# Two chained sequence models on one core: squares and sums of the norms in four parts, projections between the heads of the second model's mixers, and the last expert's residual handed over by pairs

## What is computed

```python
proj = h @ w_in
c_q, c_kv, k_rope, q_m, k_m, v_m, o_m, i_m, f_m, g_mla, g_mlstm = jnp.split(proj, split_at, axis=-1)
q = (_rmsnorm(c_q, q_norm_w) @ w_uq)...          # 8 heads, 64 + 32 (rotated)
kv = (_rmsnorm(c_kv, kv_norm_w) @ w_ukv)...      # 8 heads, 64 + 64
y_mla = _mla_attention(q_nope, q_rope, k_nope, k_rope, v)
qk = jax.nn.silu(_causal_dwconv(jnp.concatenate([q_m, k_m], axis=-1), conv_w, conv_b))
hm = _mlstm_chunkwise(q_m, k_m * 64 ** -0.5, v_m, i_pre, log_sigmoid(f_pre))
y_mlstm = jax.nn.sigmoid(o_m) * _rmsnorm(hm, head_norm_w)
merged = (jax.nn.sigmoid(g_mla) * (y_mla @ w_br_mla)
          + jax.nn.sigmoid(g_mlstm) * (y_mlstm @ w_br_mlstm))
return merged @ w_out
```

## Time and profile before

| | |
|---|---|
| time, three runs | 2615.55 us median, 2609.03 to 2618.73 |
| profiled execution | 2614.95 us |
| its span in the trace | 2613.1 us, mean granted clock 0.933 |
| TensorE busy | 2408.3 us (92%), 12979 matmul records |
| VectorE, ScalarE busy | 1620.1 us (62%), 1102.9 us (42%) |
| weights and inputs read | 575.26 MB, 221 GB/s over the span |
| second model's mixers | from 1473.66 to 1801.06 us and from 2046.06 us to 2374.4 us of the span |

### The profile page before, as it was taken

How to read it: one execution, slowest core, us unless ns; L and a number is a source line. 1 busy time by engine, 2 the same in 40 slices (tenths; PEclk the granted TensorE clock), 3 DMA queues, 4 the chain that set the end, 5 groups by cost and what they waited for, 6 DMA issues and landing times.

```text
span 2613.1 us, 31144 instructions
## 1 busy us (share of the span) xinstructions
PE 2408.3 (92%) x12979; PEld 2074.1 (79%) x12979; DVE 1620.1 (62%) x1728; ACT 1102.9 (42%) x1187; POOL 54.2 (2%) x101
## 2 busy tenths in 40 slices
PE   1988998987999999999999799998999999898997
PEld 1777998776888888888888686687898786687996
DVE  3574875335898898898899232423888223334674
ACT  0233442415666676766666122112444122113552
POOL 1000000000000000000000000000000000000000
PEclk9979998987999999999999996699999895899998
DMA  8753986423999999999999451043887350143551
GB/s 283 268 192 108 335 303 222 145 81 128 369 377 366 360 378 372 356 376 373 374 365 369 118 151 33 15 146 99 310 276 234 98 162 1 49 145 98 193 184 42
DMA packets 338882, 578.38 MB, mean 221 GB/s; under 512 B 48082, under 2 KB 208810, under 8 KB 326450
## 3 DMA queue, kind: packets, MB, share of 16 engines
q1 hardware_dynamic: 324738, 474.65, 53.2%
q0 software_dynamic: 13824, 100.67, 9.9%
q10 hardware_dynamic: 176, 1.02, 0.1%
HBM read 575.26 MB, written 1.05 MB: 221 GB/s over the span
## 4 chain that ended last, share of the span: by engine, by line
PE 81%; DVE 10%; ACT 5%; issue 2%; SPq 2%; DMA 1%; DVEq 0%; ACTq 0%
PE bank L515 79%; ACT arena L1281 2%; DVE w_low L1689 2%; SPq L405 2%; DVE arena L1697 1%; DVE ada_acc L1697 1%; DVE x L1697 1%; PE bank L1068 1%; ACT w_hi L1281 1%; ACT L1281 1%; DVE arena L1765 1%; DVE arena L1689 1%; DMA ring<-in_moe_w 1%; DVE arena L1915 1%; PE bank L819 0%
## 5 line engine op out<-in xcount | busy, mean ns | idle before, releaser
L1689 DVE TENSOR_TENSOR w_low<-ring,moe_w_hi 128x2048 fp32r<-128x2048 f32 x264 | 594.5, 2284 | 12.6 <-ACT moe_w_hi L1281 12.4
L1281 ACT ACTIVATE moe_w_hi<-ring 128x2048 fp32r<-128x2048 f32 x264 | 506.2, 1918 | 199.2 <-DMA ring<-in_moe_w 149.0
L515 PE MATMUL bank<-h,ring 128*128 128x256 f32 (+2 forms) x2208 | 498.1, 389 | 30.8 <-ACT h L1281 14.1
L515 PEld LDWEIGHTS bank<-h,ring 128*128 128x128 f32 (+2 forms) x2208 | 420.5, 191 | 107.1 <-issue 20.0
L515 PE MATMUL bank<-moe_w_hi,hx_hi 128*128 128x512 f32 (+1 forms) x768 | 287.1, 380 | 2.0 <-DVE hx_low L1689 2.0
L515 PE MATMUL bank<-h_hi,w_hi 128*128 128x256 f32 x1056 | 266.4, 290 | 18.7 <-ACT h L1281 12.9
L515 PE MATMUL bank<-moe_w_hi,hx_low 128*128 128x512 f32 (+1 forms) x768 | 283.4, 375 | 0.0
L515 PE MATMUL bank<-h_hi,w_low 128*128 128x256 f32 x1056 | 261.7, 284 | 0.0
L1281 ACT ACTIVATE arena<-bank 128x512 f32<-128x512 f32 (+2 forms) x182 | 94.1, 519 | 381.1 <-PE bank L515 353.2
L515 PEld LDWEIGHTS bank<-h_hi,w_hi 128*128 128x128 f32 x1056 | 201.2, 191 | 27.6 <-issue 12.7
L515 PEld LDWEIGHTS bank<-h_hi,w_low 128*128 128x128 f32 x1056 | 203.7, 193 | 0.0
(11 more groups left out here) (168 smaller groups left out, 3331.9 us busy)
## 6 DMA issues: line engine op xcount, KB each, us to landing
ring<-in_moe_w SPq DMA_DIRECT2D x264, 1024.0 KB, 7.2
ada_in<-in_ada_w POOLq DMA_DIRECT2D x96, 1024.0 KB, 7.3
ring<-in_w_in SPq DMA_DIRECT2D x56, 1024.0 KB, 5.4
ring<-in_ffn_w_up SPq DMA_DIRECT2D x44, 1024.0 KB, 6.4
ring<-in_ffn_w SPq DMA_DIRECT2D x33, 1024.0 KB, 6.3
ring<-in_ffn_w_down SPq DMA_DIRECT2D x22, 1024.0 KB, 5.1
ring<-in_w_out SPq DMA_DIRECT2D x16, 1024.0 KB, 5.1
ring<-in_w_br_mla SPq DMA_DIRECT2D x4, 1024.0 KB, 5.1
```

Source lines behind the costliest of these rows:

```text
L515: ins = nc.tensor.matmul(out, lhsT, rhs, start=start, stop=stop, skip_group_check=shared)
L1281: return nc.scalar.activation(out, in_, f, **kw)
L1689: return nc.vector.tensor_tensor(out, a, b, op)
```

## The change

Four things are changed.

First, the norms: the square is four instructions of 512 columns, each behind its own two counts of x_ready, and TensorE waits for norm_sq before every second matmul of the sum. The sum goes to bank 1 instead of bank 7.

Second, in mixer2 twelve projection units stand in other places. The second half of vm, the four gmla and two gml units stand in the steps of the attention, one a step, the last in two halves over two steps. The other two gml units and the two om units stand as halves in the eight steps of the mLSTM. ScalarE only copies these banks, and takes the sigmoids later in three large instructions (gm1, om, gm2). The em rows are selected, and the gate rows transposed, before the attention, and outputs has one instruction less. The last head's values come after the first mLSTM products.

Third, the tail of mixer2: the head norm is done in halves, brmla's first unit stands before the second half, brml's first block takes its input by halves (yml_ready), and w_out's first block takes h by pairs (ycat_ready). The banks of these stages are others, the memory places too, and the loads follow in the new order (om after gml).

Fourth, after the last expert x_ready rises by 2 after each pair.

```diff
             def norm_sum():
-                need("norm_sq")
-                fill(7)
+                fill(1)
...
+                    if kb % 2 == 0:
+                        need("norm_sq")
+                    mm(bank[1][:, 0:T], ones, sq[:, kb, :], start=(kb == 0), stop=(kb == KB - 1),
...
-                project_tokens("vm", li, (2, 4), "z_v")
-                project_bank(("om", li, 0), 5, "z_outgate")
-                project_bank(("om", li, 1), 6, "z_outgate")
...
+                def beside_attention(step):
+
+                    if step == 0:
+                        project_values(li, 1, 6)
+                    elif step < 5:
+                        project_bank(("gmla", li, step - 1), 6, "z_gm")
+                    elif step == 5:
+                        project_bank(("gml", li, 0), 6, "z_gm")
+                    else:
+                        project_half(("gml", li, 1), 6, step - 6, "z_gm")
...
                         modulation(5, MOD_PARTS[1][0] + 4 * step, MOD_PARTS[1][0] + 4 * step + 4)
-                    if 1 <= step < 9:
+                        beside_attention(step)
+                    if step >= 1:
                         weighted(step - 1)
...
+                def beside_mlstm(step):
+
+                    unit, i = divmod(step, 2)
+                    key = (("gml", li, 2), ("gml", li, 3), ("om", li, 0), ("om", li, 1))[unit]
+                    project_half(key, (3, 5)[unit % 2], i, "z_gm" if key[0] == "gml" else "z_outgate")
...
                 for step in range(9):
                     if step < 8:
                         log_weights(step)
                         products(step)
+                        if step == 0:
+                            values(7)
+                        beside_mlstm(step)
+                    else:
+                        head_sum(0, 3)
                     if step >= 1:
                         combine(step - 1)
...
+                            if kind == "brml" and j == 0 and i == 0 and kb % 2 == 0:
+                                need("yml_ready")
...
+                branch("brmla", 0, yla, (0, 7))
+                head_sum(1, 2)
+                branch("brmla", 1, yla, (5, 1))
+                branch("brml", 0, yml, (6, 3))
+                branch("brml", 1, yml, (4, 2))
+                for j, b in enumerate((0, 5, 3, 7)):
                     fill(b)
...
+                    project(("wout2", li, j), b, KB, hk, 2, per_kb=None if j else "ycat_ready", inc="wout_psum")
...
-                need("x_ready", KB)
-                sq = region(0, KB * T)
-                tell(func(sq, x[:, :, :].rearrange("p k t -> p (k t)"), ACT.Square), "norm_sq")
+                for j in range(KB // 2):
+                    need("x_ready", 2)
+                    func(region(j * 2 * T, 2 * T), x[:, 2 * j:2 * j + 2, :].rearrange("p k t -> p (k t)"),
+                         ACT.Square).then_inc(s["norm_sq"], 1)
...
+                head_std(0, 3)
+                tell(func(M2["gm1"], M2["gm1"], ACT.Sigmoid), "gm_sb")
+                tell(func(M2["om"], M2["om"], ACT.Sigmoid), "outgate_sb")
+                need("hm_ready", 2)
+                tell(func(M2["hsq"][:, 512:1024], M2["hm"][:, 512:1024], ACT.Square), "headsq_sb")
+                tell(func(M2["gm2"], M2["gm2"], ACT.Sigmoid), "gm_sb")
+                head_std(1, 2)
...
                         ins.then_inc(s["moe_added"], 1)
+                        if e == EXPERTS - 1:
+                            dve.wait_ge(s["moe_added"], 4 * e + j + 1)
+                            dve.sem_inc(s["x_ready"], 2)
...
-                dve.wait_ge(s["moe_added"], 4 * EXPERTS)
-                dve.sem_inc(s["x_ready"], KB)
```

More of the change, by code:

```diff
@@ L920, in mixer2, with branch @@
-                project_out("wout2", li, (2, 4, 6, 7))
+                def branch(kind, j, y, banks):
+                    arrive((kind, li, j))
+                    w = slot_view((kind, li, j), 4, 512)
+                    for i in range(4):
+                        b = banks[i // 2]
+                        if i % 2 == 0:
+                            fill(b)
+                        for kb in range(4):
+                            if kind == "brml" and j == 0 and i == 0 and kb % 2 == 0:
+                                need("yml_ready")
+                            mm(bank[b][:, (i % 2) * T:(i % 2 + 1) * T], w[:, kb, i * P:(i + 1) * P], y[:, kb, :],
+                               start=(kb == 0), stop=(kb == 3), inc="z_br" if i % 2 and kb == 3 else None)
+                    owed.append(1)
@@ L1474, in turned, with beside_attention @@
                     tell(func(pt, bank[b][:, 0:384], ACT.Copy), "attT_sb", b)
+                def beside_attention(step):
+                    if step == 0:
+                        token_values(1)
+                    elif step < 6 or step == 7:
+                        unit = min(step, 6) - 1
+                        need("z_gm")
+                        tell(func(region(unit * 512, 512), bank[6][:, :], ACT.Copy), None, 6)
+                token_values(0)
                 for step in range(9):
@@ L1986, in mixer2 @@
                 tell(tt(M2["qro"], M2["qro"], M2["qr"], ALU.add), "rot_sb")
+                need("atok_psum")
+                tell(nc.vector.tensor_copy(small[:, 112:128], bank[5][:, 0:16]), None, 5)
                 def masked(head):
                     need("att_psum")
-                    o = (head % 2) * 512
+                    o = (head % 2) * 384
                     b = head % 2
@@ L2018, in attended @@
                              "yla_sb", b)
-                for step in range(10):
-                    if 1 <= step < 9:
+                for step in range(9):
+                    if 1 <= step:
                         normalised(step - 1)
@@ L2028, in mixer2 @@
                 modulation(2 + li, 1, 5)
-                need("atok_psum")
-                tell(nc.vector.tensor_copy(small[:, 112:128], bank[5][:, 0:16]), None, 5)
                 def log_weights(head):
```

247 lines of the change are left out of this document (132 added, 115 removed).

## The result

The changed kernel takes 2508.59 us, the median of four runs (2506.21 to 2513.12), against 2616.41 us for the kernel before beside it (2609.03 to 2618.73, four runs): a ratio of 0.9595 with an interval of 0.9571 to 0.9618. That is 108 us or 4% less. Predicted were 2501, in a range of 2487 to 2530. The profiled execution took 2506.21 us; its span is 2504.4 us, 108.7 less than before, at a mean granted clock of 0.961 instead of 0.933.

The account below looks back on a forecast made before the run. TensorE, busy 92% of the span, was taken as the bound, mostly by its half clock in the heads. Mixers 86.9, norms 25.6 and pairs 1.5 make 114.0 us: 2614.95 - 114.0 = 2501, eight in ten 2487 to 2530.

Parts of the forecast that it names:

- Rival (b): Both head stages: the clock falls in nearly every step, at most 2547 us, attention alone 2518; range 2513 to 2547, chance 0.20.
- (a): Attention: the clock stays up throughout, 12 us less, 2489 us; chance 0.66 together with the forecast (2487 to 2513).
- Only the last head has less, about 5.6 us, and may leave 0.2 us idle: Attention: cover for a head's masking, exponential and normalising; other heads have a whole step, 11.2 us or 7.7 with a half unit.
- Clock falls here: none taken: mLSTM heads with half units between them: no time lost to clock falls.
- the waits on VectorE would vanish: mLSTM: the combine no longer waits for VectorE's outputs, which need 25.49 us in a stage of 53 us.
- The 0.6 us at brml: Mixer tail: brml's third matmul waits 0.3 to 1 us for the gated heads' second half; 0.6 taken, 1.2 for both.
- 6 us a mixer: Attention: cost of clock falls beside the heads, the middle between 0 and 14.4 us a mixer.
- 1.9 each: Norms before the second mixer and the first model's second layer: the sum ends at 2040.6 instead of 2042.5, 3.8 us together.
- 3.8: Norm after the first model's final norm: squares run along, its sum ends at 1466.3 instead of 1470.1, saving 3.8 us.
- 1.5: Last expert's x_ready by pairs: saves nothing if TensorE is leaving the branch, otherwise up to 3.4 us; 1.5 taken.
- The last norm: End of the kernel: squares run along with the residuals, the sum ends near 2595.1 instead of 2599.8, saving 4.7 us.
- no idle over 0.3 us in a step: Sign of being right: in no step of the attention or mLSTM is TensorE idle over 0.3 us.

Follow-up runs that it names:

- ahead: The changed kernel with the first mLSTM head's log_weights and products before the last attention head's transposes; 2502.63 us, ratio 0.9563 to the kernel before.
- mlstm_apart: The changed kernel with the mLSTM's eight half units taken out of the steps and put together in its first step; 2528.08 us, 0.9649.
- both_apart: The changed kernel with the attention's units before its first head and the mLSTM's eight halves together in its first step; 2580.49 us, 0.9847.
- pairs_undone: The changed kernel with x_ready raised once, by 8, after the last expert; 2507.3 us, 0.9572.
- nobranch: The changed kernel without the choice between gathered and dense experts: the gathered form always runs, the dense form is left out; 2504.66 us, 0.9561.
- mod_last: The changed kernel with the modulation's 32 one-column matmuls moved out of the attention's steps to before the last head's transposes; 2516.06 us, 0.9607.

## Why the prediction was right, and where its steps were not

**The attention.** The terms were 49 us of units at their old price, 33.7 for the heads at full clock and 6 for the clock: 88.7. The stretch is 88.83: 49.0, 5.1 for three falls, 1.66 idle, and so 33.1 for the heads, without the last head's values (0.8), which come in the mLSTM now. The price of a head from the few pieces at the stage's start held to 2%. By the ratio near 2 of the two formulas in the Trainium skill, "TensorE: Matmul & The Clock Gate", Back-to-back issue gap, a head is 3.9 us, an estimate. The prediction read them as a stream's time; the section gives them as the gap of single matmuls, too low where columns are few. Measured are 4.21 us, and between full and half clock a ratio of 1.84, so this trace doesn't agree with the ratio of 2. Rival (b), a fall in nearly every step, is excluded at three of eight; (a), none, as well.

**The last head.** The step that failed is "Only the last head has less, about 5.6 us, and may leave 0.2 us idle". The cover was counted from the head's own chain. VectorE's order was left out: an older copy stood ahead of the normalisation. The trace of the kernel before already had this wait of 1.66 us, as part of the 4.53 idle us that the prediction took as saved in full. The wait is 1.66 us in each mixer, and in the second the clock fell behind it: 59.4 us from 2157.84 to 2217.22 against 56.15, 3.2 more. With the wait taken out (ahead) the stages are 4.3 us shorter on average.

**The mLSTM.** By the terms 28 + 25.1 = 53.1 us, measured 56.15. The half units cost 3.65 and not 3.5 us each (1.2 for eight), and two pieces moved in from elsewhere: the last head's values (0.8) and the first of the two head sums (1.0), which stood in the tail before. "Clock falls here: none taken" held in the first mixer, where the stretch is at 1.00, and failed in the second, where the clock fell behind the last head's wait. That the waits on VectorE would vanish was right; mlstm_apart has them back.

**The tail.** The 0.6 us at brml did not come: the branches run without a gap. It was the difference of two sums of about 16 us each, so within their error. VectorE has the second half of the gated heads ready at 1706.4, 15.8 us after the last combine (16.1 by the prediction), and just then TensorE comes to the third matmul. w_out and the sum behind it came as priced: from w_out's end to the sum's end 3.5 us (1747.39 to 1750.85) instead of 6.8, so 3.4 for 3.0.

**The clock beside the heads.** 6 us a mixer were taken, the middle between two bounds; that it came near is luck as much as method, since the same instructions cost between 5.1 and 8.3 us of clock in these traces. The falls in the heads' stages are 5.1 us in the first mixer and, with the one behind the wait, 8.3 in the second. Beyond them the first stretch of the first mixer ran 2.6 us longer than before, at 0.95 instead of 1.00, and the same stretch of the second 3.3 us shorter, at 1.00 instead of 0.95. Of the 4.5 us that the first mixer saved less than forecast, the start is 2.6 and the mLSTM 3.0, with 1.3 back from the tail, which gave up a head sum, and from the stage up to the heads.

**The norms.** 25.6 and 1.5 predicted, 28.0 measured by the table, but two terms were wrong by 4 us in opposite directions. At the second layer of the first model "1.9 each" became 5.6, since the idle 2.99 us in front of it are gone and the sum ran at full clock:

```profile
429.98 3.70 PE L516 MATMUL bank<-arena,const 128*128 128x256 f32 x16
```

Before, it took 6.14 us. Part of this is luck: the same sum behind the same instructions takes 5.39 us in ahead, both_apart and pairs_undone, which leaves 3.9 of the 5.6. Behind the experts "3.8" and "1.5" became 1.3 and nothing. The sums there ran slower than before, near half clock (6.63 and 6.45 us against 5.14 and 5.62 of the earlier trace rows), and the 4.67 us of "issue" remained. The prediction had named the case, "If that time is TensorE coming out of the branch, pieces give nothing", and taken 1.5 between the two. With nobranch the wait is gone, so it belongs to the branch and its code, and this term of 1.5 us should have been nothing. The last norm came as priced:

```profile
2485.65 5.38 PE L516 MATMUL bank<-arena,const 128*128 128x256 f32 x16 [1.88 <-ACT arena L1333]
```

**The signs.** Of the signs that the prediction named, the attention stretch (88.8 us in both mixers, 0.94 in the first), the first mLSTM (56.15) and the idle before the sums behind w_out came. Not met were no idle over 0.3 us in a step (1.66 at the last head), the wait at brml, and 54 to 58 us in the second mLSTM (59.4). In the table the mixers fall 6.2 us short of their terms, and the rest saves 0.9 more than its own.

**What stays open.** What decides where a fall of the clock comes to lie. From the sum of the norm in front of a mixer to the first scores it is 95.8 us in the changed kernel's first mixer and 92.4 in its second; other runs with the same instructions there have 92.4 to 96.0. With the heads' stages (145.0 to 148.2) this makes differences of some 3 us a mixer in places that no edit touches. So pairs_undone at 0.9572, with an interval that overlaps that of the changed kernel, shows no gain of its edit, and what nobranch gains by its ratio beyond the 6.6 us isn't attributed either.

## What to carry to other kernels

Where small matmuls hold TensorE at half clock, put full projections between them in pieces: here that was worth 40 us in the two attentions. The projections between the mLSTM's heads brought 14 to 18 us, the smaller part of that stage's gain. Read a wait together with the pieces behind it, since one of 1.7 us cost up to 5 more in clock. And when a chain's cover is counted, walk the queue of the engine that does the work, and not the chain alone: what stands ahead of it there may wait for work that another engine does later. Look for the wait in the trace of before, too: this one stood there with the same length.

## What the runs showed of the hardware

A piece of eight one-column records takes 1.05 us at full clock and 1.87 at half, and a head as a whole 4.21 and 7.75: ratios of 1.8 for a halved clock. The clock fell two or three times in a stage of 7 us units and 4.2 us heads (changed kernel, pairs_undone), and in mod_last, where the heads between the units take 3.3 us, at none of the units in either mixer. Behind the experts' branch TensorE's first instruction comes after 4.4 to 5.4 us without a releaser in all runs that have the branch, although in the changed kernel the squares that it needs are done 2.8 us before it; without the branch 1.0 to 1.8 us are left, which have a named releaser.
